# Modulation products with features on partitions: one multiply-and-sum per 128 features, all slots in the first two layers

## The chip, the cores and the metric

The kernel runs on one core of a Trainium2 chip. The metric is the time of one execution on the device in microseconds (us). All data are 32-bit floats. Five engines work side by side and are tied together by semaphores: TensorE (PE; its weight loads are PEld), VectorE (DVE), ScalarE (ACT), GpSimd (POOL) and SyncE (SP), which here issues the loads.

## The reference

Four transformer layers run over one sequence of 256 tokens with 1024 features: a gated-MLP layer, a chunked-attention layer, an "even" layer (forgetting and sliding-window attention) and an "odd" layer (sparse attention and eight experts). The last two are modulated by a vector `c`:

```python
def ada_modulation(c, w, b):                      # c [1, 1024], w [1024, 6144]
    mod = jax.nn.silu(c) @ w + b
    return jnp.split(mod[:, None, :], 6, axis=-1)

def even_layer(x, c, ...):                        # odd_layer likewise
    sh_m, sc_m, g_m, sh_f, sc_f, g_f = ada_modulation(c, ada_w, ada_b)
    h = rms_norm(x, norm_mix) * (1 + sc_m) + sh_m
    ...
    x = x + g_m * mix
    h = rms_norm(x, norm_ffn) * (1 + sc_f) + sh_f
    return x + g_f * swiglu(h, ffn_gate, ffn_up, ffn_down)
```

The two modulation matrices hold 6144 x 1024 numbers each, 50 MB together. Neither depends on the tokens.

## The kernel before

**The stream.** All weights come as one list of slots, each up to 128 x 2048 numbers (1 MB), in the order in which they are used. `Plan` writes the list. SyncE loads slot s into `raw[s % 6]` (`load`, L371); before it reuses a place it waits until TensorE has used the weights there (`w_used`) or, for a modulation slot, until VectorE is done with it (`lo_done`). ScalarE rounds a weight slot to its high part (`whi`, L1135), VectorE subtracts it to get the low part (`wlo`, `split`, L1679). TensorE makes each product as three matmuls (L449 to L451) from the high and low parts of activations and weights. A product of 512 columns from 1024 rows takes two weight slots; a "chunk" is such a product for both halves of 128 tokens.

**The order of the stages** is gmlp_in, gmlp_out, up0, down0 (the first layer's feed-forward block), kv, q, attn_out, up1, down1, e_in, e_out, e_up, e_down (even layer), o_in, o_out and the experts.

**Modulation slots** ("a") stand between the weight slots, at the places that `behind` names for each stage. There are 48 of them, 24 for each modulated layer. Slot n of a layer holds four blocks of 128 rows of the matrix for 512 output features, so two slots make 512 features. When `split` has made the low part of the weight slot in front of it, it calls `modulate`, which multiplies the rows on the partitions by silu(c) and adds: four operations of 128 x 512 into `acc` (L1703, L1705), each waiting for the one before. The sum over the 128 partitions is left to TensorE: `ada_turn` waits for the second slot of the pair and makes four matmuls of `acc` with a column of ones into bank 4 of PSUM (L665). `ada_cols` (L1727) adds the bias and stores 512 features as four columns of 128. Because bank 4 serves other purposes as well, the spatial product and the second scores of each attention wait for `ada_taken`. Of the 48 slots, 24 stand in the first two layers (none in up0 and up1) and 24 in e_in, e_out, e_up and e_down.

**The feed-forward block of the first two layers** (`conv_ffn`, `gated_ffn`). up0 and up1 are eleven chunks each. In one turn of the loop ScalarE copies the finished chunk out of PSUM (L1189), TensorE turns it (L614), ScalarE makes the convolution's first tap (L1285), VectorE adds two more taps in eight operations (L1930), ScalarE takes Silu (L1290), VectorE multiplies and splits (L1941, L1944, L1945). VectorE's instructions run in the order of the program: the low parts of the next chunk's two slots come first in a turn, then the convolution of the chunk before. down0 and down1 take 12 weight slots; the last low parts for them are interleaved with the last two turns of the convolution, and the first of these stand in this order:

```python
evac()                                    # low parts of the first two slots of down
convolve(j, lambda: split(used[0] + LEAD))     # the third, between taps and products
split(used[0] + LEAD + 1)                      # the fourth
convolve(n - 1, lambda: split(used[0] + LEAD + 2))   # the fifth
```

**Normalised projections.** Into e_in, e_up and o_in (`residual_normed`, `normed_product`) TensorE waits until VectorE and ScalarE have added the residual, normalised and scaled the first half of the tokens. VectorE adds the first half (t = 0) when that half of the last slot's product is done (`t0_done`); ahead of it it splits two more weight slots.

Of the kernel before, what the change touches and what calls it, by code (L numbers as in the profile page):

```python
# [22 lines left out]
ALU = mybir.AluOpType  # L23
# [54 lines left out]
C_C = C_AB + 2 * 6 * KT  # L78
C_END = C_C + KT

# [20 lines left out]
class Plan:  # L101
# [3 lines left out]
    def __init__(self):  # L105
        self.width, self.kind, self.q, self.at, self.qat, self.ada = [], [], [], {}, {}, []
        self.nq = 0
        left = [ADA, ADA]

        def add(widths, layer=None, behind=()):  # L110
            for i, w in enumerate(widths):
# [4 lines left out]
                if i in behind:  # L116
                    n = ADA - left[layer]
                    left[layer] -= 1
# [3 lines left out]
                    self.ada.append((len(self.kind) - 1, layer, n))  # L122
# [4 lines left out]
        def proj(name, n, order=None, kt=KT, layer=None, behind=(), first=None):  # L127
# [5 lines left out]
            add([k * w for (_, w), ks in zip(chunks_of(n, order), parts) for k in ks], layer, behind)  # L133
# [14 lines left out]
        assert not left[0]  # L148
# [4 lines left out]
        assert not left[1]  # L153
# [37 lines left out]
def build_program(nc, x_in, cols_in, rows_in, vg_in, fg1_in, fg_in, pos_in, ws_in, toep_in, rw_in, stream_in, out):  # L191
# [3 lines left out]
    with ctx:  # L195
# [35 lines left out]
        cs = sb("cs", [P, KT])  # L231
        acc = sb("acc", [P, W])
# [110 lines left out]

        neg_max, total, sink, weight = ((lambda u, t, c=c: sx[:, u // 4 % 2, c, t, u % 4:u % 4 + 1]) for c in range(4))
        parts = lambda t: slice(t * P, t * P + (t + 1) * P)

        def turned_before(name):

            return sum(n % 2 for s, _, n in PL.ada if s < AT[name])

# [2289 lines left out]
```

## Time and profile before

| what | us |
|---|---|
| median of 3 runs | 1512.16 |
| lowest and highest run | 1512.07, 1515.78 |
| span of the profiled execution, first to last instruction | 1509.6 |
| median of the runs, beyond that span | 2.6 |
| TensorE busy in the span | 1447.0 |
| VectorE busy | 1220.9 |
| ScalarE busy | 899.8 |
| data moved | 356.15 MB, 236 GB/s on the mean |

The page gives no time for the profiled execution but its span, so the sum further down is made against the span. Times in the profile are counted from the span's start. "Busy" leaves out waits; matmuls overlap, so a matmul's duration (0.39 us for 512 columns) is longer than the time to the next one (0.23 us). The stages follow each other: up0 begins at 93 us, down0 at 224, kv at 290, q at 340, attn_out at 391, up1 at 416, down1 at 547, e_in at 618, e_up at 734, e_down at 865 and o_in at 936 us.

### The profile page before, as it was taken

To read this page: it belongs to the slowest core of one execution; us is meant where nothing else is said; L and a number is where in the kernel's file an instruction comes from. 1 tells how busy PE (TensorE), PEld (TensorE's weight loads), DVE (VectorE), ACT (ScalarE), POOL (GpSimd) and SP (SyncE) were. 2 spreads that over 40 slices of the span, in tenths; PEclk is the share of its full clock that TensorE was granted. 3 is DMA by queue.
4 is the path that set the end of the run, shared out by engine and by line. 5 is a ranking of instruction groups with operands and counts; after the bars stand their busy time and mean duration, and the time that the engine had idled before them with its cause. 6 is when DMAs were issued, how large, how long until landed. Compare 5 with 4: busy or idle time off the path is not lost.

```text
span 1509.6 us, 19548 instructions
## 1 busy us (share of the span) xinstructions
PE 1447.0 (96%) x7128; PEld 1186.0 (79%) x7129; DVE 1220.9 (81%) x1664; ACT 899.8 (60%) x1207; POOL 5.6 (0%) x18
## 2 busy tenths in 40 slices
PE   6999999999999999998999999979899999999996
PEld 5888888887688887886788887856788888888885
DVE  6776879767767889878878788697688998999897
ACT  6555664556656563567433334547676777787774
POOL 0000000000000000000000000000000000000000
PEclk9999999999999999999999999979899999999999
DMA  8565446875355457561576676421289898998883
GB/s 298 226 231 187 169 172 231 331 269 222 112 199 188 157 181 294 212 247 58 200 272 253 261 314 239 162 89 61 118 324 340 329 337 319 340 354 324 330 332 152
DMA packets 53422, 356.15 MB, mean 236 GB/s; under 512 B 6096, under 2 KB 7120, under 8 KB 12896
## 3 DMA queue, kind: packets, MB, share of 16 engines
q1 hardware_dynamic: 52592, 352.15, 62.7%
q0 software_dynamic: 320, 2.65, 0.5%
q8 instruction: 49, 0.80, 0.2%
q10 hardware_dynamic: 432, 0.30, 0.1%
q14 instruction: 29, 0.24, 0.0%
HBM read 354.03 MB, written 1.05 MB: 235 GB/s over the span
## 4 chain that ended last, share of the span: by engine, by line
PE 77%; DVE 13%; ACT 6%; DMA 2%; issue 2%; SPq 0%; DVEq 0%; ACTq 0%
PE ps L449 23%; PE ps L451 22%; PE ps L450 22%; DVE wlo L1679 4%; DMA raw<-stream_dram 2%; PE ps L614 1%; ACT attn_scratch L1321 1%; PE ps L541 1%; ACT whi L1135 1%; PE ps L665 1%; DVE acc L1705 1%; DVE tok L1930 1%; ACT tok L1342 1%; DVE xlo L1769 1%; DVE tok L1864 1%
## 5 line engine op out<-in xcount | busy, mean ns | idle before, releaser
L1679 DVE TENSOR_TENSOR wlo<-raw,whi 128x2048 fp32r<-128x2048 f32 (+2 forms) x302 | 645.2, 2163 | 90.4 <-ACT whi L1135 79.0
L1135 ACT ACTIVATE whi<-raw 128x2048 fp32r<-128x2048 f32 (+2 forms) x302 | 541.1, 1816 | 173.9 <-DMA raw<-stream_dram 169.0
L449 PE MATMUL ps<-whi,xhi 128*128 128x512 f32 (+3 forms) x1360 | 533.8, 392 | 14.1 <-DVE xlo L1859 4.2
L451 PE MATMUL ps<-whi,xlo 128*128 128x512 f32 (+3 forms) x1360 | 522.5, 384 | 0.0
L450 PE MATMUL ps<-wlo,xhi 128*128 128x512 f32 (+3 forms) x1360 | 521.8, 384 | 0.0
L449 PEld LDWEIGHTS ps<-whi,xhi 128*128 128x128 f32 x1360 | 256.8, 189 | 70.4 <-issue 8.0
L451 PEld LDWEIGHTS ps<-whi,xlo 128*128 128x128 f32 x1360 | 256.9, 189 | 51.4
L450 PEld LDWEIGHTS ps<-wlo,xhi 128*128 128x128 f32 x1360 | 257.4, 189 | 46.5
L449 PE MATMUL ps<-whi,ahi 128*128 128x512 f32 x440 | 176.5, 401 | 1.4 <-DVE wlo L1679 1.3
L451 PE MATMUL ps<-whi,alo 128*128 128x512 f32 x440 | 173.7, 395 | 0.0
L450 PE MATMUL ps<-wlo,ahi 128*128 128x512 f32 x440 | 173.6, 395 | 0.0
L1705 DVE SCALAR_TENSOR_TENSOR acc<-raw,cs,acc 128x512 f32<-128x512 f32 x168 | 126.2, 751 | 5.1
L1930 DVE SCALAR_TENSOR_TENSOR tok<-ps,cols,tok 128x255 f32<-128x255 f32 (+1 forms) x176 | 72.7, 475 | 41.1 <-ACT tok L1285 40.3
L449 PEld LDWEIGHTS ps<-whi,ahi 128*128 128x128 f32 x440 | 83.0, 189 | 22.1 <-issue 2.6
L451 PEld LDWEIGHTS ps<-whi,alo 128*128 128x128 f32 x440 | 82.9, 188 | 19.2
L450 PEld LDWEIGHTS ps<-wlo,ahi 128*128 128x128 f32 x440 | 83.0, 189 | 17.8
L1189 ACT ACTIVATE tok<-ps,st 128x512 f32<-128x512 f32 x64 | 40.5, 685 | 55.5 <-PE ps L614 35.9
L1290 ACT ACTIVATE tok<-tok 128x512 f32<-128x512 f32 x22 | 13.9, 632 | 65.6 <-DVE tok L1930 65.6
L1554 ACT ACTIVATE tok<-ps 128x256 f32<-128x256 f32 (+1 forms) x48 | 17.4, 363 | 49.6 <-PE ps L451 49.4
L1285 ACT ACTIVATE tok<-ps,cols 128x256 f32<-128x256 f32 x88 | 42.5, 575 | 3.8 <-DVEq L1948 3.8
L1321 ACT ACTIVATE attn_scratch<-attn_scratch,sx 128x128 f32<-128x128 f32 x80 | 35.3, 445 | 10.0 <-DVE sx L2011 9.9
L1305 ACT ACTIVATE tok<-ps 128x512 f32<-128x512 f32 x11 | 6.6, 598 | 52.9 <-PE ps L451 52.9
(316 smaller groups left out, 1166.1 us busy)
## 6 DMA issues: line engine op xcount, KB each, us to landing
raw<-stream_dram SPq DMA_DIRECT2D x315, 1024.0 KB, 4.9
raw<-stream_dram SPq DMA_DIRECT2D x32, 512.0 KB, 3.9
attn_scratch<-toep_dram POOLq DMA_DIRECT2D x1, 2048.0 KB, 11.7
raw<-stream_dram SPq DMA_DIRECT2D x2, 528.0 KB, 4.5
h<-x_dram SPq DMA_DIRECT2D x2, 512.0 KB, 4.7
y<-tok SPq DMA_DIRECT2D x4, 256.0 KB, 2.7
head_scratch<-w_s_dram SPq DMA_DIRECT2D x1, 512.0 KB, 13.9
head_scratch<-vg_dram SPq DMA_DIRECT2D x1, 512.0 KB, 11.0
```

The costliest lines, as they stand in the source:

```text
L449: pe.matmul(o, xh, wh, start=start, stop=False)
L450: pe.matmul(o, xh, wl, start=False, stop=False)
L451: return pe.matmul(o, xl, wh, start=False, stop=stop)
L541: last = pe.transpose(trb(n % 2)[0:src.shape[1], k - r, t * P:(t + 1) * P], src, ident[:, :])
L1135: act.activation(whi[:, q % SPL, 0:w], raw[:, s % RAW, 0:w], ACT.Copy).then_inc(sem("hi_done"), 1)
L1189: m = act.activation(dst[:, t], src[:, t], func, scale=st[:, 6 + t:7 + t])
L1285: m = act.activation(conv[:, f, :], ps[:, 6 + f // 2, (f % 2) * S:(f % 2 + 1) * S], ACT.Identity, scale=sc, bias=bi)
L1321: m = act.activation(x, x, ACT.Exp, bias=neg_max(u, t), scale=-1.0, accum_out=total(u, t))
L1554: act.activation(sgx[:, 0:m], ps[:, (2, 0, 1)[j % 3], m:2 * m], ACT.Silu).then_inc(sem("x_silu"), 1)
L1679: dve.tensor_tensor(low(q)[:, 0:w], raw[:, s % RAW, 0:w], whi[:, q % SPL, 0:w].bitcast(F32), ALU.subtract).then_inc(sem("lo_done"), 1)
L1705: m = dve.scalar_tensor_tensor(acc[:, :], wk, cs[:, kk:kk + 1], acc[:, :], ALU.mult, ALU.add)
L1930: m = dve.scalar_tensor_tensor(o, src, cols[:, c:c + 1], o, ALU.mult, ALU.add)
```

## The change

A modulation slot now holds two blocks of 128 output features for all 1024 rows, features on the partitions and rows along them. silu(c) is kept as a row of 1024 on every partition (`c_row`, in the half of `gates` that is free in these layers), loaded by one more broadcast DMA behind slot 8, and taken through Silu by ScalarE at the head of `conv_ffn(0)`. Each block is one `tensor_tensor_reduce` of 128 x 1024, which multiplies, sums along the row, starts from the bias and writes one column of `shf2`, `scl2` or `gcol`. The product itself is written over the slot.

TensorE's part goes (`ada_turn`, its semaphores, its waits in front of the spatial product and the scores), and so do `acc`, `ada_cols`, `take_cols` and the deferral of a slot at the end of attention (`hold`, `owed`). `1 + scale`, times the norm's gain, is made once for all, behind the last slot; the gate turns wait for `modulated`. All 48 slots stand in the first two layers: 10 in up0, 8 in down0, 8 in kv, 3 in q, 11 in up1 and 8 in down1. gmlp_in, gmlp_out, attn_out and all stages of the even layer have none.

```diff
-        proj("gmlp_in", 2 * D, G_ORDER, layer=0, behind=(4, 5), first=FIRST)
-        proj("gmlp_out", D, layer=0, behind=odd)
-        proj("up0", 2 * FF)
-        proj("down0", D, kt=FK, layer=0, behind=(4, 5, 7, 8, 10, 11))
-        proj("kv", 2 * D, layer=0, behind=(2, 3, 5, 7))
-        proj("q", D, layer=0, behind=(1, 2))
-        proj("attn_out", D, layer=0, behind=odd)
-        proj("up1", 2 * FF)
-        proj("down1", D, kt=FK, layer=0, behind=(4, 5, 7, 8, 10, 11))
-        proj("e_in", E_IN, E_ORDER, layer=1, behind=(3, 5, 7, 8))
-        proj("e_out", D, layer=1, behind=odd)
-        proj("e_up", 2 * FF, layer=1, behind=odd[1:])
-        proj("e_down", D, kt=FK, layer=1, behind=(1, 2, 4, 5, 7, 8, 10, 11))
+        early = (0, 1, 2, 3, 4, 6, 7, 8)
+        proj("gmlp_in", 2 * D, G_ORDER, first=FIRST)
+        proj("gmlp_out", D)
+        proj("up0", 2 * FF, behind=odd[1:])
+        proj("down0", D, kt=FK, behind=early)
+        proj("kv", 2 * D, behind=range(8))
+        proj("q", D, behind=range(3))
+        proj("attn_out", D)
+        proj("up1", 2 * FF, behind=odd)
+        proj("down1", D, kt=FK, behind=early)
+        proj("e_in", E_IN, E_ORDER)
+        proj("e_out", D)
+        proj("e_up", 2 * FF)
+        proj("e_down", D, kt=FK)
...
+                if s == 8:
+                    sp.dma_start(c_row, c_in.to_broadcast([P, D])).then_inc(sem("c_landed"), 16)
...
-                    ada_turn(PL.s_of[q] + 1)
...
-            def ada_turn(s):
-                if (s, turned[0] // (ADA // 2), 2 * (turned[0] % (ADA // 2)) + 1) not in PL.ada:
-                    return
-                if turned[0]:
-                    pe.wait_ge(sem("ada_taken"), turned[0])
-                pe.wait_ge(sem("lo_done"), s + 1)
-                for j in range(4):
-                    m = pe.matmul(ps[:, 4, j:j + 1], acc[:, j * P:(j + 1) * P], ones[:, 0:1], start=True, stop=True)
-                m.then_inc(sem("ada_cols"), 1)
-                turned[0] += 1
...
+                if layer == 0:
+                    act.wait_ge(sem("c_landed"), 16)
+                    act.activation(c_row, c_row, ACT.Silu).then_inc(sem("cs"), 1)
                 evac(first=True)
...
-                    act.activation(cs[:, :], cols[:, C_C:C_C + KT], ACT.Silu).then_inc(sem("cs"), 1)
...
             def modulate(s):
...
                 dve.wait_ge(sem(f"landed{s % RAW}"), 16 * (s // RAW + 1))
-                for k in range(4):
-                    kk = 4 * (n % 2) + k
-                    wk = raw[:, s % RAW, k * W:(k + 1) * W]
-                    if kk == 0:
-                        m = dve.tensor_scalar(acc[:, :], wk, cs[:, 0:1], None, ALU.mult)
-                    else:
-                        m = dve.scalar_tensor_tensor(acc[:, :], wk, cs[:, kk:kk + 1], acc[:, :], ALU.mult, ALU.add)
-                    if k < 3 or n % 2 == 0:
-                        link(m)
...
+                for b in range(2):
+                    blk = 2 * n + b
+                    part, kind, k = blk // (3 * KT), blk // KT % 3, blk % KT
+                    wk = raw[:, s % RAW, b * D:(b + 1) * D]
+                    at = C_AB + layer * 6 * KT + blk
+                    m = dve.tensor_tensor_reduce(wk, wk, c_row, 1.0, cols[:, at:at + 1], ALU.mult, ALU.add,
+                                                 (shf2, scl2, gcol)[kind][:, layer, part, k:k + 1])
+                m.then_inc(sem("lo_done"), 1)
+                if seen[0] == 2 * ADA:
+                    dve.wait_ge(sem("lo_done"), s + 1)
+                    for part in range(2):
+                        at = (C_GEM, C_GEF)[part]
+                        x = scl2[:, :, part, :]
+                        g = cols[:, at:at + 4 * KT].rearrange("p (l r) -> p l r", l=2)[:, :, 0:KT]
+                        m = dve.scalar_tensor_tensor(x, x, 1.0, g, ALU.add, ALU.mult)
+                    m.then_inc(sem("modulated"), 1)
...
-                split(used[0] + 2, hold=True)
+                split(used[0] + 2)
```

## Rows read from the trace of the kernel before

**Rows 1.** The page: busy time, GB/s in 40 slices, chain that ended last.
```profile
PE 1447.0 (96%) x7128; PEld 1186.0 (79%) x7129; DVE 1220.9 (81%) x1664; ACT 899.8 (60%) x1207; POOL 5.6 (0%) x18
...
GB/s 298 226 231 187 169 172 231 331 269 222 112 199 188 157 181 294 212 247 58 200 272 253 261 314 239 162 89 61 118 324 340 329 337 319 340 354 324 330 332 152
...
PE 77%; DVE 13%; ACT 6%; DMA 2%; issue 2%; SPq 0%; DVEq 0%; ACTq 0%
```
**Rows 2.** Waits from 126.48 to 221.47 us: total, times, longest.
```profile
DVE tok L1930 <- ACT tok L1285: 10.5, 8, 1.4
```
**Rows 3.** Stretches: length, then busy us of each engine, clock, DMA share, GB/s.
```profile
126.48:221.47 94.99, 94.99 (x450) 78.85 (x449) 76.89 (x104) 58.67 (x73) 0.00 (x0) 1.00 0.49 172
290.16:340.03 49.87, 49.61 (x242) 40.96 (x241) 34.16 (x40) 27.99 (x36) 1.49 (x2) 1.00 0.79 296
1057.00:1120.00 63.00, 57.01 (x281) 47.66 (x281) 45.93 (x66) 41.59 (x54) 0.53 (x1) 0.92 0.53 203
```
**Rows 4.** VectorE's timeline, one turn in up0: start, length, idle before.
```profile
126.48 4.50 DVE L1679 TENSOR_TENSOR wlo<-raw,whi 128x2048 fp32r<-128x2048 f32 x2
132.19 3.34 DVE L1930 SCALAR_TENSOR_TENSOR tok<-ps,cols,tok 128x255 f32<-128x255 f32 x8 [1.22 <-ACT tok L1285]
...
138.25 4.49 DVE L1679 TENSOR_TENSOR wlo<-raw,whi 128x2048 fp32r<-128x2048 f32 x2
```
**Rows 5.** VectorE's timeline where down0 begins.
```profile
221.47 3.43 DVE L1679 TENSOR_TENSOR wlo<-raw,whi 128x1024 fp32r<-128x1024 f32 x2
227.19 3.34 DVE L1930 SCALAR_TENSOR_TENSOR tok<-ps,cols,tok 128x255 f32<-128x255 f32 x8 [2.30 <-ACT tok L1285]
...
247.90 2.29 DVE L1679 TENSOR_TENSOR wlo<-raw,whi 128x2048 fp32r<-128x2048 f32 x1
```
**Rows 6.** Groups by form: count, then busy us, mean ns, idle before.
```profile
L1705 DVE SCALAR_TENSOR_TENSOR acc<-raw,cs,acc 128x512 f32<-128x512 f32 x168 | 126.2, 751 | 5.1
...
L1679 DVE TENSOR_TENSOR wlo<-raw,whi 128x1024 fp32r<-128x1024 f32 x32 | 39.1, 1223 | 6.1 <-ACT whi L1135 4.5 <-DVE alo L2401 0.9
...
L665 PE MATMUL ps<-ones,acc 128*128 128x1 f32 x192 | 22.7, 240 | 0.0
...
L1703 DVE TENSOR_SCALAR acc<-raw,cs 128x512 f32<-128x512 f32 x24 | 11.5, 479 | 0.0
```
**Rows 7.** TensorE's timeline around one column group in down0.
```profile
270.85 0.95 PE L665 MATMUL ps<-ones,acc 128*128 128x1 f32 x8
271.65 0.48 PE L449 MATMUL ps<-whi,ahi 128*128 128x512 f32 x1
```
**Rows 8.** Timelines at two exits: last matmul of the first half, VectorE's add.
```profile
723.59 0.39 PE L451 MATMUL ps<-whi,xlo 128*128 128x512 f32 x1
...
726.63 0.69 DVE L1790 TENSOR_TENSOR tok<-ps,gates 128x512 f32<-128x512 f32 x1
...
927.09 0.39 PE L451 MATMUL ps<-whi,alo 128*128 128x512 f32 x1
...
928.52 0.69 DVE L1790 TENSOR_TENSOR tok<-ps,gates 128x512 f32<-128x512 f32 x1
```
**Rows 9.** VectorE's timeline: `tensor_tensor_reduce` (add, minimum) in the chunked attention.
```profile
361.76 0.29 DVE L2011 CUSTOM_DVE_ANT_0 attn_scratch<-ps,attn_scratch 128x128 f32<-128x128 f32 x1 [0.63 <-PE ps L690]
...
361.98 0.42 DVE L2011 CUSTOM_DVE_ANT_0 attn_scratch<-ps,attn_scratch 128x256 f32<-128x256 f32 x1
362.32 0.08 DVE L2011 DVE_READ_ACCUMULATOR2_ANT sx<- 128x1 f32 x1
362.32 0.28 DVE L2011 CUSTOM_DVE_ANT_0 attn_scratch<-ps,attn_scratch 128x128 f32<-128x128 f32 x1
```
**Rows 10.** TensorE's timeline at the second slot of q.
```profile
347.50 0.50 PE L449 MATMUL ps<-whi,xhi 128*128 128x512 f32 x1 [1.29 <-DVE xlo L1769]
```
**Rows 11.** ScalarE's timeline ahead of up0.
```profile
90.37 1.06 ACT L1142 ACTIVATE tok<-h 128x1024 f32<-128x1024 f32 x1 [0.52 <-DVE h L1788]
...
98.06 1.28 ACT L1224 ACT_TABLE_LOAD   x1
```
**Rows 12.** DMA issues: count, KB each, us to landing.
```profile
attn_scratch<-toep_dram POOLq DMA_DIRECT2D x1, 2048.0 KB, 11.7
...
head_scratch<-vg_dram SPq DMA_DIRECT2D x1, 512.0 KB, 11.0
```

More of the change, by code:

```diff
@@ L107, in __init__, with add @@
         self.nq = 0
-        left = [ADA, ADA]
-        def add(widths, layer=None, behind=()):
+        def add(widths, behind=()):
             for i, w in enumerate(widths):
@@ L132, in proj @@
                 parts[0] = first
-            add([k * w for (_, w), ks in zip(chunks_of(n, order), parts) for k in ks], layer, behind)
+            add([k * w for (_, w), ks in zip(chunks_of(n, order), parts) for k in ks], behind)
         def expert():
@@ L692, in scores, with first_scores, attention @@
                 m.then_inc(sem("att_s"), 1)
-            def first_scores(units, name):
+            def first_scores(units):
                 pe.wait_ge(sem("acc_free"), T("acc"))
                 scores(units, 0)
-                cols_made = turned_before(name)
-                if cols_made:
-                    pe.wait_ge(sem("ada_taken"), cols_made)
                 scores(units, 1)
-            def attention(units, name, sm, pT, after=None, mid=None, between=lambda: None):
+            def attention(units, sm, pT, after=None, mid=None, between=lambda: None):
                 n = len(units) // 2
@@ L783, in spatial @@
                     pe.wait_ge(sem("acc_free"), 3)
-                    pe.wait_ge(sem("ada_taken"), 1)
                     for g in range(KT):
@@ L830, in last_queries @@
                 pe.wait_ge(sem("tr_free"), T("tr"))
-            attention(CHUNKED, "attn_out", SM_C, PT_C, lead(2), between=last_queries)
+            attention(CHUNKED, SM_C, PT_C, lead(2), between=last_queries)
             gated_ffn(4, rest(3))
@@ L861, in fox_heads @@
                     pe.wait_ge(sem("tr_free"), T("tr", 1))
-                    first_scores(EVEN, "e_out")
+                    first_scores(EVEN)
             def fox_keys():
@@ L871, in _ @@
             proj(width[4], after=fox_heads)
-            attention(EVEN, "e_out", SM_E, PT_E, between=fox_keys)
+            attention(EVEN, SM_E, PT_E, between=fox_keys)
             gated_ffn(2, normed=True)
@@ L1663, in _, with split @@
             seen = [0]
-            owed = [None]
-            def split(n, i=None, per=0, hold=False):
-                if owed[0] is not None:
-                    modulate(owed[0])
-                    owed[0] = None
+            def split(n, i=None, per=0):
                 while pos[0] < min(n, top[0]):
@@ L1681, in split @@
                     if s + 1 < len(PL.kind) and PL.kind[s + 1] == "a":
-                        if hold and pos[0] == n:
-                            owed[0] = s + 1
-                        else:
-                            modulate(s + 1)
+                        modulate(s + 1)
             def modulate(s):
-                _, layer, n = PL.ada[seen[0]]
-                assert PL.ada[seen[0]][0] == s
+                at, layer, n = PL.ada[seen[0]]
+                assert at == s
+                if seen[0] == 0:
+                    dve.wait_ge(sem("cs"), 1)
@@ L2150, in _ @@
             dve.wait_ge(sem("bias_ready"), 1)
-            attention(CHUNKED, "attn_out", SM_C, PT_C)
+            attention(CHUNKED, SM_C, PT_C)
             residual_then()
@@ L2190, in _ @@
             T.up("tr", 11)
-            attention(EVEN, "e_out", SM_E, PT_E)
+            attention(EVEN, SM_E, PT_E)
             residual_normed(KT, 0, 0, 1)
```

75 lines of the change are left out of this document (17 added, 58 removed).

## The prediction

> **What bounds the kernel now.** I read the page first, then the waits of one long stage, then that stage's timeline on VectorE, then the two ends of each feed-forward block. The page [rows 1] says that TensorE is busy 96% of the span and that the chain which ended last lies on it for 77% and on VectorE for 13%. So work taken off TensorE is nearly all worth its length, and work given to VectorE counts only where the chain runs through VectorE. The question is where that is.
>
> In the first feed-forward block, from 126.48 to 221.47 us, TensorE is busy 94.99 of 94.99 us and VectorE 76.89 [rows 3]. That looks like 18 us of room on VectorE. It isn't. The timeline [rows 4] shows one turn of the loop, two weight slots long: two `wlo` subtractions, an idle stretch, eight convolution steps, a short wait for Silu, three short steps, and at 138.25 the next `wlo`. The 94.99 us hold 8 turns, 11.87 each. The waits [rows 2] tell what the idle time is: 10.5 us in 8 times, 1.31 us a turn, until ScalarE has made the convolution's first tap, and that is the only part which a later VectorE could use up. The other idle pieces come behind VectorE's own work and move with it. Each `wlo` that starts a turn ends right as TensorE comes for it: both loops are equally long. Work put into a turn is free up to 1.31 us and costs its full length beyond.
>
> The end of such a block is tighter still. From 221.47 to 247.90 VectorE alternates `wlo`, convolution and products, with one idle stretch, the 2.30 us at 227.19 [rows 5], and TensorE starts on each slot as it is finished.
>
> **What is taken away.** Each of 24 output blocks of 512 features has its partial products summed across partitions by four matmuls with one column (`ada_turn`), recorded as 192 [rows 6]. One group takes 0.80 us of TensorE, from 270.85 to 271.65, where the next weights start [rows 7]. All 24 would be 19.2 us. Four of them win nothing by themselves: those ahead of the three normalised projections, where TensorE waits for VectorE anyway, and the one in `gmlp_in`, behind which the next start is set by the chain that makes `vn_ready`. 20 remain: **-16.0**.
>
> The three exits into a normalised projection get shorter too, as no modulation slot is in the way there. In `e_out` VectorE comes to the add at 726.63, right behind its last `wlo`, although the half of the product that the add reads was done at 723.98; at `e_down` the add comes at 928.52 and the half is done at 927.48 [rows 8]. An add follows a finished product by some 0.2 us, so 2.4 us and 0.8 us go. The exit of `down1` is built like that of `e_down` and its `wlo` waits for a weight slot behind two modulation slots: I count 1.1. Together **-4.3**.
>
> **What VectorE gets.** Two products of 128x1024 for each of 48 slots, in place of four of 128x512 (0.78 us from start to start, 0.751 long, so 3.05 to 3.1 a slot) [rows 6]. The same operation is in the trace at 128 and 256 elements: behind each other they start 0.22 and 0.34 us apart, the accumulator's readout included [rows 9]. That is about 0.135 us for each 128 more, so 0.22 + 7 x 0.135 = 1.16 us for 1024, and **2.3 us a pair** (call it p). The upper bound is two full lengths, 1.223 for a two-input product of that size [rows 6] and 0.08 for the readout: 2.61. The lower bound, were it to run like a one-input operation, is 1.5, as 512 elements of those took 0.48 against the 0.75 of the two-input ones [rows 6]. I take 2.3, since the row is the same operation.
>
> The Trainium skill (VectorE: DVE Perf Modes, The DRAIN you can't avoid) says that the next operation doesn't start until the pipeline is empty. The trace disagrees for this operation: one that lasts 0.42 us is followed after 0.34. By the page a pair would cost 2.61 and the sum below would be 8 us longer.
>
> **Where it gets them.** The slots move: none before `up0`, then 10, 8, 8, 3, 0, 11 and 8 in `up0`, `down0`, `kv`, `q`, `attn_out`, `up1` and `down1`, and none after.
>
> *`up0` and `up1`.* They had none. Now one stands behind the second slot of nearly each turn, between `wlo` and the convolution: 2.3 - 1.31 = 0.99 us a turn. Eight turns of each block are in the tight loop; the others fall in its start, where VectorE is idle for 7 us. 2 x 8 x 0.99 = **+15.8**. Nothing later gives it back: TensorE can't start a slot before its `wlo`.
>
> *`down0` and `down1`.* Five slots stand right behind the first five weight slots. The first two, 4.6 us, fall before the idle 2.30 and cost 2.3; the next two cost 2.3 each; the fifth replaces one that was there before (3.05, ahead of the `wlo` at 247.90) and wins 0.75. That makes 5p - 5.35 = 6.15 us for each, **+12.3**. The three in the second half have room: the `wlo` there is 2 to 6 us early.
>
> *`kv` and `q`.* In `q` a slot now precedes the split of the activations. TensorE was already held there, 1.29 us before its second slot, by that split [rows 10]; two pairs of 2.3 take the place of one group of 3.05: +1.6. In `kv` the stream is one modulation slot for each weight slot, 8 of each, beside the 2 MB of the bias table [rows 12]: 18.9 MB in about 47 us, 400 GB/s, where this stretch now moves 296 GB/s [rows 3] and the page's best slice shows 354 [rows 1]. At 1.05 MB a slot that is 53 us at 354; the six-slot ring hides some. +3 (0 to 6). Together **+4.6**.
>
> *The silu of c*, now 128x1024 on ScalarE at the head of `up0`, before two weight copies: 1.28 for a table and some 1.06 for the operation, as another one of that size takes [rows 11], of which some half is covered, as `wlo` there was about 1 us early: **+1.2**. The one in `gmlp_in` that goes had room behind it. The load of c itself lies among loads that land long before use: nothing. If that cover were gone it would be the 11.0 us that the like load of `vg` takes [rows 12]. The waits for `ada_taken` ahead of the scores and the spatial product go with the groups. The last two operations, which turn all scales at once, are a few tenths on VectorE in `down1`'s second half, with room.
>
> **Sum.** -16.0 - 4.3 + 15.8 + 12.3 + 4.6 + 1.2 = +13.6 us. The profiled execution's span is 1509.6, so 1523.2; the median of the runs, 1512.16, lies 2.6 above that span, and the prediction is **1525.8 us**. As a function of p the sum is 26p - 46 (16 turns and five slots in each of two block ends): each tenth of a us on a pair is 2.6 us, it is zero at p = 1.77, and +21.6 at 2.61.
>
> **The rivals.**
> 1. *Faster: the product fits into the wait.* Were a pair 1.5 us, the turns would cost 0.2 each and the sum were -7: 1505. It decides at 1.77 us a pair. For it: the operations with one tensor input do run faster. Against: this one reads two, and its own rows give 0.135 us per 128. A sum below zero could also come of a smaller loss at the ends of the blocks. 12%.
> 2. *No change: the ends of the blocks don't lose.* Were `down0` and `down1` to take the five slots without a loss, because TensorE's wait for the last hidden blocks moves no further, the sum is +1: 1513. Against it: VectorE has no idle time there but the 2.30. 13%.
> 3. *Each product pays its full length*, p = 2.61, or the stream in `kv` costs 9 us more than counted here: 1534. This is also what the page on VectorE gives. Against it: [rows 9]. 15%.
> 4. *The clock falls.* TensorE would be busy 11.75 of 12.86 us a turn, 91%. In [rows 3] a stretch with 90% (57.01 of 63) showed a granted clock of 0.92. A clock of 0.92 would lengthen a turn's TensorE work to 12.8, just what the turn lasts; only below that does it cost, some 1 us a turn at 0.85, so 16 turns make 1541. 5%.
> The forecast has 55%, its own range 1519 to 1531.
>
> **The numbers.** A measurement can tell about 0.3%, 4.5 us, from no change. Faster by more than that (below 1507.6): 12%. Within: 15%, rival 2 and part of the forecast's low side. Slower: 73%. The range from 1511 to 1537 leaves out rival 1 and the far side of 3 and 4.
>
> **What would show it.** The second product of a pair starts 1.16 us behind the first, and 2.3 us lie between `wlo` and the next operation. In `up0` and `up1` the wait of the convolution for ScalarE is gone from VectorE, the turn is 12.86 us instead of 11.87, and TensorE waits about 1 us a turn for `wlo`. `up0` with `down0` takes 14 us more up to the start of `down0`'s second half, and so does `up1` with `down1`. From the end of `down1` to the start of `o_in`'s product the kernel is 12 us shorter: 10 groups and the three exits. Wrong it would be if the pair is far from 2.3, if `kv` starves on the stream, or if TensorE's clock falls in the feed-forward blocks.

## The result, and the profile after

The changed kernel takes 1527.98 us (median of 4 runs, 1527.58 to 1528.86); the kernel before, beside it, 1512.24 (1512.07 to 1515.78). The ratio is 1.0104, with an interval from 1.0087 to 1.0122: it is slower by 1%. The prediction was 1525.8 us, slower.

The page of the changed kernel, as in [rows 1] and [rows 6]:

```profile
PE 1434.2 (94%) x6936; PEld 1165.9 (76%) x6937; DVE 1198.1 (78%) x1634; ACT 895.8 (59%) x1205; POOL 5.6 (0%) x18
...
PE 64%; DVE 24%; ACT 6%; issue 4%; DMA 2%; SPq 0%; DVEq 0%; ACTq 0%
...
L1667 DVE CUSTOM_DVE_ANT_0 raw<-raw,gates,cols 128x1024 f32<-128x1024 f32 x96 | 119.2, 1279 | 0.0
```

TensorE has 12.8 us less to do and VectorE 22.8 us less. The program is 15.7 us longer all the same, because VectorE's share of the chain that ended last has risen from 13 to 24%: its work was made smaller and put where nothing covers it. The timeline of VectorE shows it for one turn in up0, the turn of [rows 4]:

```profile
139.21 4.49 DVE L1649 TENSOR_TENSOR wlo<-raw,whi 128x2048 fp32r<-128x2048 f32 x2
143.62 1.28 DVE L1667 CUSTOM_DVE_ANT_0 raw<-raw,gates,cols 128x1024 f32<-128x1024 f32 x1
144.82 0.08 DVE L1667 DVE_READ_ACCUMULATOR2_ANT shf<- 128x1 f32 x1
144.82 1.28 DVE L1667 CUSTOM_DVE_ANT_0 raw<-raw,gates,cols 128x1024 f32<-128x1024 f32 x1
146.03 0.08 DVE L1667 DVE_READ_ACCUMULATOR2_ANT shf<- 128x1 f32 x1
146.03 3.33 DVE L1875 SCALAR_TENSOR_TENSOR tok<-ps,cols,tok 128x255 f32<-128x255 f32 x8
...
152.09 2.29 DVE L1649 TENSOR_TENSOR wlo<-raw,whi 128x2048 fp32r<-128x2048 f32 x1
```

The pair takes from 143.62 to 146.03, 2.41 us; the convolution follows without the idle time that it had in [rows 4]; the turn lasts 12.88 us (139.21 to 152.09) instead of 11.87, the mean of the eight turns in [rows 3]. TensorE's waits over eight such turns (139.21 to 242.30 us), and its busy time there:

```profile
PE ps L442 <- DVE wlo L1649: 8.0, 8, 1.6
```
```profile
139.21:242.30 103.09, 95.10 (x448) 77.69 (x446) 95.89 (x138) 58.02 (x73) 0.00 (x0) 1.00 0.65 250
```

TensorE was busy for all of the 94.99 us in [rows 3]. For the same work it now needs 103.09, of which 95.10 are work and 8.0 are eight waits for `wlo`. The granted clock is 1.00, the upper of its two levels (2.4 GHz): it isn't the clock.

**Where the 17.5 us of span went.** I compared the time at which TensorE starts on each weight slot in both traces. The shift at a stage's start, after minus before: up0 -1.2, down0 +7.4, kv +12.4, q +15.3, attn_out +13.8, up1 +13.0, down1 +21.5, e_in +26.4, e_up +22.3, e_down +18.0, o_in +14.3, o_out's last slot +15.9, end of the program +17.5. Between neighbouring slots the shift gives each term:

| term | predicted | measured |
|---|---|---|
| column groups off TensorE | -16.0 | -16.9 |
| exits of down1, e_out, e_down | -4.3 | -4.3 (1.05, 2.35, 0.88) |
| up0 and up1, up to the first slot of down0, down1 | +15.8 | +14.7 (7.6, 7.1) |
| first half of down0 and down1 | +12.3 | +15.4 (7.5, 7.9) |
| kv and q | +4.6 | +3.0 |
| silu of c | +1.2 | +1.0 |
| second slot of up1 | 0 | +1.3 |
| half clock in o_in | 0 | +1.6 |
| the experts | 0 | +1.6 |
| sum | +13.6 | +17.4 |

The first half of down0 in VectorE's timeline, which answers to [rows 5]:

```profile
229.76 1.22 DVE L1649 TENSOR_TENSOR wlo<-raw,whi 128x1024 fp32r<-128x1024 f32 x1
230.90 1.28 DVE L1667 CUSTOM_DVE_ANT_0 raw<-raw,gates,cols 128x1024 f32<-128x1024 f32 x1
...
233.31 2.29 DVE L1649 TENSOR_TENSOR wlo<-raw,whi 128x2048 fp32r<-128x2048 f32 x1
...
237.93 3.33 DVE L1875 SCALAR_TENSOR_TENSOR tok<-ps,cols,tok 128x255 f32<-128x255 f32 x8
...
262.80 3.43 DVE L1649 TENSOR_TENSOR wlo<-raw,whi 128x2048 fp32r<-128x2048 f32 x2
```

VectorE has no idle time here. It begins the block 8.29 us later than before (229.76 against 221.47) and makes the low part that stood at 247.90 [rows 5] at 262.80, 14.90 later: 6.6 us for five slots, as 5p - 5.35 = 6.7 says at p = 2.41. TensorE's first start in down0 moved by only 7.4, since that low part had been 1.0 us early. So 0.9 us of each block end in the table belongs to the turns: 16.5 for the turns and 13.6 for the two ends. In down1 VectorE's part was 6.4 us (sixth low part at 571.02 before, at 599.79 now; start of the block 22.37 later); some 0.6 us more came from a stretch at half clock, shown in the last section.

The last two rows of the table don't come from anything that the change edits. From o_out's last slot to the end, which is the experts, the two kernels do the same, in 452.5 us before and 454.2 now. It took between 451.1 and 456.9 in the eight kernels up to `old_clear` below, whichever way their slots lay, and 451.1 and 454.7 in two executions of one and the same kernel (`old_clear`); a profile of one execution cannot tell 2 us there from nothing.

### The profile page after: what moved, and what is told of

Read it like the earlier page. It is cut to its first block, busy times and chain, and to the rows that moved or that the text cites. A ratio compares the mean times of both kernels' runs of the same rounds, so it can differ in the third digit from the quotient of the medians.

```text
span 1527.1 us, 19080 instructions
## 1 busy us (share of the span) xinstructions
PE 1434.2 (94%) x6936; PEld 1165.9 (76%) x6937; DVE 1198.1 (78%) x1634; ACT 895.8 (59%) x1205; POOL 5.6 (0%) x18
## 3 DMA queue, kind: packets, MB, share of 16 engines
HBM read 354.55 MB, written 1.05 MB: 233 GB/s over the span
## 4 chain that ended last, share of the span: by engine, by line
PE 64%; DVE 24%; ACT 6%; issue 4%; DMA 2%; SPq 0%; DVEq 0%; ACTq 0%
PE ps L442 19%; PE ps L444 19%; PE ps L443 19%; DVE wlo L1649 7%; DVE tok L1875 5%; DVE raw L1667 5%; DMA raw<-stream_dram 2%; ACT attn_scratch L1298 1%; PE ps L533 1%; ACT whi L1109 1%; DVE alo L1890 1%; DVE tok L1886 1%; ACT tok L1264 1%; DVE ahi L1889 1%; ACT tok L1319 1%
## 5 line engine op out<-in xcount | busy, mean ns | idle before, releaser
L442 PE MATMUL ps<-whi,xhi 128*128 128x512 f32 (+3 forms) x1360 | 534.1, 393 | 32.1 <-DVE wlo L1649 16.5
L1667 DVE CUSTOM_DVE_ANT_0 raw<-raw,gates,cols 128x1024 f32<-128x1024 f32 x96 | 119.2, 1279 | 0.0
L1927 DVE TENSOR_TENSOR tok<-ps,tok 128x512 f32<-128x512 f32 x11 | 7.6, 692 | 46.1 <-ACT tok L1282 41.3
```

The lines of the kernel that those rows point to most:

```text
L442: pe.matmul(o, xh, wh, start=start, stop=False)
L1667: m = dve.tensor_tensor_reduce(wk, wk, c_row, 1.0, cols[:, at:at + 1], ALU.mult, ALU.add, (shf2, scl2, gcol)[kind][:, layer, part, k:k + 1])
```

## The experiments

**`one_product`: the second product of a pair cut to 8 of its 1024 rows, in up0 and up1 alone.** (The kernel leaves out the rest of these sums, so some modulation values are incomplete.)

```diff
+                    short = b and (AT["up0"] <= s < AT["down0"] or AT["up1"] <= s < AT["down1"])
+                    r = slice(0, 8 if short else D)
-                    m = dve.tensor_tensor_reduce(wk, wk, c_row, 1.0, cols[:, at:at + 1], ALU.mult, ALU.add,
+                    m = dve.tensor_tensor_reduce(wk[:, r], wk[:, r], c_row[:, r], 1.0, cols[:, at:at + 1], ALU.mult, ALU.add,
```

> In up0 and up1 the second product of each modulation slot runs over 8 of its 1024 rows only; loads, order and all else are as in the changed kernel (some modulation values are therefore partial sums). Theory A (a turn of the loop costs what VectorE gets beyond the 1.31 us in which it waited before): a pair takes some 2.34 us in the changed kernel, here about 1.17 + 0.17 = 1.34, so the turn falls from 12.9 to about 11.9 us and the time by 16 x 1.0 = 16 us, to 1512 us. Rival B (the third slot of the stream in each turn, its transfer and its place in the ring, makes the turn longer): the turn stays at 12.9 and the time at 1528 us.

Measured: 1510.21 us (1507.41 to 1513.27, 10 runs) beside 1513.09 for before; ratio 0.9982, 0.9971 to 0.9994. VectorE's timeline of a turn, then TensorE's waits over eight turns (138.07 to 233.00 us):

```profile
138.07 4.49 DVE L1649 TENSOR_TENSOR wlo<-raw,whi 128x2048 fp32r<-128x2048 f32 x2
142.48 1.28 DVE L1669 CUSTOM_DVE_ANT_0 raw<-raw,gates,cols 128x1024 f32<-128x1024 f32 x1
...
143.68 0.22 DVE L1669 CUSTOM_DVE_ANT_0 raw<-raw,gates,cols 128x8 f32<-128x8 f32 x1
...
143.96 3.34 DVE L1877 SCALAR_TENSOR_TENSOR tok<-ps,cols,tok 128x255 f32<-128x255 f32 x8
...
150.02 2.29 DVE L1649 TENSOR_TENSOR wlo<-raw,whi 128x2048 fp32r<-128x2048 f32 x1
```
```profile
PE ps L442 <- DVE wlo L1649: 0.5, 1, 0.5
```

One product and a stub last 1.48 us, 0.17 over the wait of 1.31, and the turns are back: 0.5 us of waits instead of 8.0. 21 shorter products are some 18 us off the time (the ratio went from 1.0104 to 0.9982), because 16 of them lay in turns that VectorE paces. It also shows the margin: half a slot fits into a turn of up0 or up1, a whole one doesn't.

**`down_late`: the slots of down0 and down1 away from the convolution.**

```diff
-        early = (0, 1, 2, 3, 4, 6, 7, 8)
+        early = range(4, 12)
```

> The eight slots of down0 and of down1 stand behind weight slots 4 to 11 in place of 0 to 4 and 6 to 8. Theory A (they cost where VectorE's low parts alternate with the last two turns of the convolution, 7.5 us in each of the two blocks by the traces): the start of the sixth weight slot moves back by 7 us in each, at the price of about 1 us at the exit of down1 and up to 5 us of waiting for the stream, which then has one modulation slot for each weight slot through the end of down0, kv and q: 1514 to 1519 us. Rival B (VectorE has too much to do in the whole of down0 and down1, wherever it stands): the loss moves to the second half, 1526 to 1528 us.

Measured: 1528.23 us (1524.61 to 1531.86, 4 runs); ratio 1.0092, 1.0073 to 1.0112, no better than the changed kernel. My time of 1514 to 1519 was missed, though its mechanism held: the first half of down0 now loses nothing (shift of TensorE's start from down0's first slot to its sixth -0.4 us instead of +7.5, and -0.6 instead of +7.9 in down1). It was given back behind: some 2.5 us at the eighth and ninth slot of each block, 3.9 at the entry of kv, 1.0 at that of q and 7.2 at the entry of e_in; 1.3 more went in q's first slot, where the clock was at half speed from 353.2 to 360.0 us (mean 0.50). The time is that of rival B, but only the 2.5 us a block lie in the second half, where B had put the loss. VectorE's timeline at that last place, in `down_late` and then in the changed kernel:

```profile
631.13 2.29 DVE L1649 TENSOR_TENSOR wlo<-raw,whi 128x2048 fp32r<-128x2048 f32 x1 [0.69 <-ACT whi L1109]
635.39 2.29 DVE L1649 TENSOR_TENSOR wlo<-raw,whi 128x2048 fp32r<-128x2048 f32 x1 [1.96 <-ACT whi L1109]
...
637.96 0.69 DVE L1733 TENSOR_TENSOR h<-ps,h 128x512 f32<-128x512 f32 x1
```
```profile
630.73 2.29 DVE L1649 TENSOR_TENSOR wlo<-raw,whi 128x2048 fp32r<-128x2048 f32 x1 [1.95 <-ACT whi L1109]
...
636.69 0.69 DVE L1733 TENSOR_TENSOR h<-ps,h 128x512 f32<-128x512 f32 x1 [3.43 <-PE ps L444]
```

In the changed kernel VectorE is through with its low parts and waits 3.43 us for TensorE, then adds at once. In `down_late` the products of the last slots have pushed the low parts behind the finished half of the product, and the residual add follows a low part with no idle time ahead of it. From TensorE's last matmul of down1 to its first product of e_in it is 12.2 us instead of 5.1.

**`clear_of_split`: no slot ahead of the split of the activations.**

```diff
-        proj("kv", 2 * D, behind=range(8))
-        proj("q", D, behind=range(3))
-        proj("attn_out", D)
-        proj("up1", 2 * FF, behind=odd)
+        proj("kv", 2 * D, behind=(0, 2, 3, 4, 5, 6, 7))
+        proj("q", D, behind=range(4))
+        proj("attn_out", D, behind=(1,))
+        proj("up1", 2 * FF, behind=odd[1:])
```

> The modulation slots behind the second weight slot of kv and of up1 are moved to the end of q and to attn_out. In the changed kernel TensorE waits 1.4 us longer than before in front of that weight slot in both stages. Theory A (the pair of products stands ahead of VectorE's split of the second half of the activations): both waits go, -2.9 us, 1525.1 us. Rival B (the longer wait is one for the weights): they stay, and the time is 1528 us within 0.5.

It was made for a wait that I hadn't predicted. In kv of the changed kernel a pair of products stands between a low part and the split of the second half of the tokens, and the second slot waits for that split; VectorE's timeline, then TensorE's:

```profile
305.84 1.28 DVE L1667 CUSTOM_DVE_ANT_0 raw<-raw,gates,cols 128x1024 f32<-128x1024 f32 x1
...
308.38 0.41 DVE L1713 CAST xhi<-tok 128x512 fp32r<-128x512 f32 x1
308.82 0.69 DVE L1714 TENSOR_TENSOR xlo<-tok,xhi 128x512 fp32r<-128x512 f32 x1
```
```profile
308.71 0.39 PE L444 MATMUL ps<-whi,xlo 128*128 128x512 f32 x1
310.63 0.50 PE L442 MATMUL ps<-whi,xhi 128*128 128x512 f32 x1 [1.54 <-DVE xlo L1714]
```

Measured: 1528.78 us (1526.83 to 1530.81, 4 runs), ratio 1.0102, 1.0083 to 1.0121: the time didn't fall by the 2.9 expected. In the trace both waits are gone (the distance between the two matmuls fell from 1.92 to 0.47 us, and likewise in up1), 2.9 us together. Most of it came back where the slots went: 0.7 at q's second slot, 0.5 at its fourth, 0.8 at the second and third slot of attn_out, which now has a modulation slot. From kv's start to up1's second slot 0.9 us are left. O_out's last slot starts 1.7 us earlier than in the changed kernel, but 1.6 of that arose in o_in, where the stretch at half clock was 3.4 us instead of 6.8 (last section), behind everything that was edited. Then the experts, which it doesn't touch, took 456.86 us against 454.15, by the stretches of the two kernels:

```profile
1071.24:1528.10 456.86, 437.05 (x2080) 361.07 (x2079) 396.73 (x375) 328.85 (x371) 0.53 (x1) 0.98 0.80 297
```
```profile
1072.95:1527.10 454.15, 435.43 (x2080) 359.90 (x2079) 397.54 (x375) 327.71 (x371) 0.53 (x1) 0.98 0.80 299
```

So the wait is real and was removed in the trace; moving its slots to these places was worth 0.9 us in the trace, and the measured time cannot tell that from nothing, since 1 or 2 us drown in the experts' scatter.

**`placed`: all 48 slots still in the first two layers, but where I thought that there was room.** Half slots in the turns of up0 and up1, down0 and down1 as in `down_late`, the rest in gmlp_in, gmlp_out, kv, q and attn_out.

```diff
+        proj("gmlp_in", 2 * D, G_ORDER, first=FIRST, behind=(8,))
+        proj("gmlp_out", D, behind=(0, 1, 2, 3))
+        proj("up0", 2 * FF, behind=(3, 5), halves=(7, 9, 11, 13, 15, 17, 19, 21))
+        proj("down0", D, kt=FK, behind=(4, 5, 6, 7, 8, 9, 10, 11))
+        proj("kv", 2 * D, behind=(0, 1, 2, 3, 4, 5, 6, 7))
+        proj("q", D, behind=(1, 2, 3))
+        proj("attn_out", D, behind=(0, 1, 2, 3))
```

> All together, the same computation: half slots (one product) in up0 and up1 except in two early turns each, eight late slots in down0 and down1, none behind the second weight slot of up1, slots in gmlp_in, gmlp_out and attn_out too, silu of c taken earlier in gmlp. Theory A (only VectorE's work beyond its idle time costs): against the changed kernel -16 for the turns, -15 for the block ends, -1.4 for up1, -1 for the silu, and up to +6 for the stream: 1495 to 1501 us, below the kernel before. Rival B (the total of VectorE's added work or the stream sets the time): above 1512 us.

Measured: 1519.95 us (1515.52 to 1524.90, 12 runs), ratio 1.0043, 1.0028 to 1.0058; slower than before, 19 us or more over what I expected. The turns did cost nothing (both blocks 0 us). The loss sits at the entries, in TensorE's waits up to the experts:

```profile
PE ps L444 <- DVE xlo L1716: 8.6, 4, 4.1
...
PE ps L557 <- DVE tok L1800: 6.1, 1, 6.1
...
PE ps L535 <- DVE h L1735: 3.1, 2, 2.1
```

The first is the split of the activations, the second the normalised half at e_in (a gap of 12.5 us there, as in `down_late`), the third a residual add ahead of up0 and another at the end of attn_out. The time is on rival B's side of 1512; the waits are those at the entries, which neither theory had. A slot at the end of one stage stands in VectorE's queue ahead of what the next stage waits for.

**`old_places`: the new operation at the places of the kernel before.** `c_row` gets a buffer of its own, so that it may live through the even layer. To make room, the convolution's coefficients move from `cols` into the free half of `gates`.

```diff
-        proj("up0", 2 * FF, behind=odd[1:])
+        proj("up0", 2 * FF)
...
+        proj("e_in", E_IN, E_ORDER, behind=(3, 5, 7, 8))
+        proj("e_out", D, behind=(1, 3))
+        proj("e_up", 2 * FF, behind=(3, 5, 7, 9, 11, 13, 15, 17, 19, 21))
+        proj("e_down", D, kt=FK, behind=(1, 2, 4, 5, 7, 8, 10, 11))
...
-        c_row = gates[:, 1, :]
+        c_row = sb("c_row", [P, D])[:, :]
+        cv = gates[:, 1, 0:C_CE]
```

> The new products at the places of the kernel before (24 slots in the first two layers, none in up0 and up1, 24 in the even layer). For that silu(c) has a buffer of its own and is made in gmlp_in as before, the convolution's coefficients lie in the second half of gates until e_in, and each layer's scales are finished behind its 24th slot; the computation is the same. Theory A (the change loses only by where the slots stand, and gains by the column groups and the shorter products): 20 groups of 0.8 us less than before, some tenths more from products of 2.42 in place of 3.1 us, 1 us back for the longer silu: 1494 to 1498 us. Rival B (the form of the products costs, through a bigger read of a shared row or the accumulator's readout): 1512 us or more.

Measured: 1490.45 us (1489.40 to 1493.33, 4 runs) beside 1512.32; ratio 0.9851, 0.9832 to 0.9871. Without the new places the change is a gain of 22 us; the places of the changed kernel turn it into a loss. It was some 5 us better than expected; `shifted`, below, shows where most of these come from.

**`old_clear`: the same, with the slots moved off the three exits, those that lead into e_in, e_up and o_in.**

```diff
-        proj("up0", 2 * FF)
-        proj("down1", D, kt=FK, behind=(4, 5, 7, 8, 10, 11))
-        proj("e_out", D, behind=(1, 3))
-        proj("e_up", 2 * FF, behind=(3, 5, 7, 9, 11, 13, 15, 17, 19, 21))
-        proj("e_down", D, kt=FK, behind=(1, 2, 4, 5, 7, 8, 10, 11))
+        proj("up0", 2 * FF, behind=(3, 5))
+        proj("down1", D, kt=FK, behind=(4, 5, 7, 8))
+        proj("e_out", D)
+        proj("e_up", 2 * FF, behind=(3, 5, 7, 8, 9, 11, 12, 13, 15, 17, 19, 21))
+        proj("e_down", D, kt=FK, behind=(1, 2, 4, 5, 7, 8))
```

(up1 has `behind=(3, 5)` too.)

> As old_places, with the slots taken away from the exits into the three normalised projections (the last two of down1 and e_down and both of e_out) and put into the loose first turns of up0 and up1 and into e_up. Theory A (the exits lose 4 us to slots that stand close to them, and the first turns of up0 and up1 take slots for nothing): 3 to 4 us less than old_places, 1491 to 1494 us. Rival B (the exits are set by the normalisation alone, or slots in up0 and up1 cost wherever they stand): no less than old_places.

Measured: 1485.60 us (1480.69 to 1486.94, 5 runs), ratio 0.9809, 0.9787 to 0.9831; run a second time, as `old_clear_again`, 1483.24 (1482.98 to 1489.41), ratio 0.9812, 0.9793 to 0.9832. VectorE's add at the exit into e_in, first `old_places`, then `old_clear`:

```profile
597.42 2.29 DVE L1653 TENSOR_TENSOR wlo<-raw,whi 128x2048 fp32r<-128x2048 f32 x1 [1.96 <-ACT whi L1112]
...
600.00 0.69 DVE L1736 TENSOR_TENSOR h<-ps,h 128x512 f32<-128x512 f32 x1
```
```profile
592.20 2.29 DVE L1653 TENSOR_TENSOR wlo<-raw,whi 128x2048 fp32r<-128x2048 f32 x1 [1.97 <-ACT whi L1112]
...
597.92 0.69 DVE L1736 TENSOR_TENSOR h<-ps,h 128x512 f32<-128x512 f32 x1 [3.19 <-PE ps L446]
```

The three gaps on TensorE are 5.1, 4.9 and 4.9 us instead of 7.4, 5.8 and 9.0: 7.3 us in all, of which the ratio shows 0.4%, 6 us. With `crow_first`, below, whose time can't be told from it, it is the fastest of the versions tried, 27 to 30 us below the kernel before.

**`shifted` and `shifted_before`: the place of two buffers.** In `old_places` TensorE made a slot of down0 in 5.49 us where the changed kernel takes 5.60, with no wait in it and the clock at 1.00. Both read `ahi` and `alo`, and moving the coefficients had put these 1408 bytes lower in each partition. These two kernels move the coefficients alone, in the changed kernel and in the one before. The small buffers behind `cols` move along; `xhi`, `xlo`, `whi`, `wlo` and `raw` stay where they are in every kernel of this document, so of what these matmuls read only `ahi` and `alo` have moved.

```diff
-C_CW = 9 * KT
+C_BS = 9 * KT
+C_CW = 0
...
         lf = sb("head_scratch", [P, FK * S])[:, :]
+        cv = sb("conv_cols", [P, C_CE])[:, :]
```

> The changed kernel, only the 352 columns of convolution coefficients stand in a buffer of their own behind the two large scratch buffers, so that ahi and alo (with the scratch) lie 1408 bytes lower in each partition, as they do in old_places and old_clear. There the matmuls that read ahi and alo follow each other 0.2289 us apart, in the changed kernel 0.2333 (TensorE's timeline, three stretches each). Theory A, it is the place of these two buffers: spacing 0.229 here too, 1320 such matmuls x 4.4 ns = 5.8 us less, of which some 1 us lies in the first halves of down0 and down1, where TensorE waits for VectorE anyway: 4.5 to 5 us shorter, 1523. Theory B, it comes from what else runs at that time (the 48 slots at other places): spacing 0.233 and 1528, as the changed kernel.

> The kernel before with the same move of the convolution coefficients: ahi and alo 1408 bytes lower than in the kernel before, where the spacing is 0.2325 us. That is another place than in old_places (before still has acc and cs ahead of them, 2080 bytes). Theory A: the spacing changes with the place, to 0.229 if this place is a good one (5 us less, 1507), or stays near 0.2325 if it is not (1512). Theory B: 0.2325 and 1512 within 1 us.

Measured: `shifted` 1522.88 us (1519.33 to 1524.94, 6 runs), ratio 1.0065, 1.0049 to 1.0082; `shifted_before` 1507.38 (1502.52 to 1514.32, 8 runs), ratio 0.9967, 0.9948 to 0.9986. TensorE's starts on two neighbouring slots of down0, in the changed kernel and in `shifted`:

```profile
279.31 0.40 PE L442 MATMUL ps<-whi,ahi 128*128 128x512 f32 x1
...
284.91 0.40 PE L442 MATMUL ps<-whi,ahi 128*128 128x512 f32 x1
```
```profile
278.85 0.39 PE L444 MATMUL ps<-whi,ahi 128*128 128x512 f32 x1
...
284.34 0.39 PE L444 MATMUL ps<-whi,ahi 128*128 128x512 f32 x1
```

24 matmuls lie between the two: 5.60 us are 0.2333 each, 5.49 are 0.2288. 1320 such matmuls (528 of them in the experts) make 6 us, which the ratios show (1.0104 to 1.0065, 0.39%). The theory that it comes of the slots' places falls. The kernel before went at 0.2321, `old_places` at 0.2289: 1320 times 3.2 ns are 4 us. So of the 22 us of `old_places` about 4 belong to the buffers' place and 18 to the operation and the groups that it takes away. The same holds of the change itself, at 0.2333 against 0.2321: some 1 us of its loss, spread over the rows of the table, is the place of two buffers and not the slots.

**`crow_first` and `crow_pad`: which place?** `old_clear` with `c_row` ahead of `ahi`, without and with 32 bytes of padding.

```diff
+        c_row = sb("c_row", [P, D])[:, :]
+        pad = sb("pad", [P, 8])
         with nc.sbuf_tensor("ahi", [P, FK, S], F32R) as ahi, nc.sbuf_tensor("alo", [P, FK, S], F32R) as alo:
...
-        c_row = sb("c_row", [P, D])[:, :]
```

> old_clear with c_row, 4096 bytes, placed ahead of ahi and alo instead of behind the scratch buffers; nothing else changes. Counted from the place of ahi in the changed kernel, the spacing of the matmuls that read ahi and alo was 0.2333 us at 0, 0.2321 at +2080 bytes (the kernel before), 0.229 at -1408 (old_clear, shifted) and 0.2267 at +672 (shifted_before). This one is at +2688. Theory A, what counts is the place modulo 2048 bytes or a divisor of it: +2688 is 32 bytes off +672, spacing near 0.227, 2 to 3 us shorter than old_clear: 1481. Rival B, what counts is something else (distance to another buffer, or a larger modulus): anything between 0.2267 and 0.2333, so 1481 to 1491. The kernel before is fixed at 1512.

> crow_first with 32 bytes of padding ahead of ahi, so that it is at +2720, 2048 bytes from the place in shifted_before (0.2267 us). Theory A (modulo 2048): spacing 0.2267 exactly as in shifted_before, 1481. If crow_first and crow_pad differ by more than 1 ns of spacing, 32 bytes matter; if both are slow, the modulus is larger than 2048 or the rule is another.

Measured: `crow_first` 1484.94 us (1479.43 to 1490.54, 5 runs), ratio 0.9804, 0.9778 to 0.9830; `crow_pad` 1488.54 (1485.23 to 1492.10, 5 runs), ratio 0.9826, 0.9807 to 0.9846. The starts on two neighbouring slots of down0, first `crow_first`, then `crow_pad`:

```profile
267.35 0.39 PE L444 MATMUL ps<-whi,ahi 128*128 128x512 f32 x1
...
272.84 0.39 PE L444 MATMUL ps<-whi,ahi 128*128 128x512 f32 x1
```
```profile
267.68 0.40 PE L445 MATMUL ps<-whi,ahi 128*128 128x512 f32 x1
...
273.28 0.40 PE L445 MATMUL ps<-whi,ahi 128*128 128x512 f32 x1
```

A slot takes 5.49 us in the first, 5.60 in the second. The intervals of the two times overlap; the pace is what tells them apart. The modulus of 2048 that I had guessed was not tested, because I had counted two of the places wrong. The kernel before has `cs` (32 bytes) and `acc` (2048) ahead of `ahi`, and its `cols` is eight columns, another 32 bytes, longer. Counted from the changed kernel, its `ahi` lies at +2112 and not at +2080, and that of `shifted_before` at +704 and not at +672. `crow_pad`, at +2720, is therefore 2016 bytes from `shifted_before`, not 2048; the test needs 64 bytes of padding and was not run. No two of the six places contradict a modulus of 2048, and none shows it beyond the pair 4096 bytes apart. What stands: 32 bytes change the pace by 2%, and two places 4096 bytes apart (`old_clear` and `crow_first`) gave the same. The rule is open.

## Why the prediction was right

It was 2.2 us low, with the likeliest case and its mechanism: VectorE's longer turns and block ends cost more than TensorE wins. Signs that it named are there: from the fourth slot of up0 to the sixth of down0 the kernel lost 15.0 us, and as much from the fourth slot of up1 to the sixth of down1, for 14 forecast; and from e_in to o_in it won the 12 that had been said. By its own steps:

- **The groups and the exits.** Both held: -16.9 and -4.3 for -16.0 and -4.3. The three exits, of which one had been costed by likeness only (1.1 us for down1), measured 1.05, 2.35 and 0.88. From e_in to o_in the kernel gained 12.1 us more, with the exit of down1 13.1; 12 had been said, 8 for ten groups and 4.3 for the exits.
- **The price of a pair.** 2.3 us was worked out from the same operation at 128 and 256 elements, and it is 2.41: the step from one start to the next is 1.21 us, not 1.16. That it came so near is in part luck. The starts in [rows 9] are 0.22 and 0.34 us apart, which is 0.12 for each 128 more and not 0.135; from 0.12 a pair is 2.1 and the sum +9, 1521. From 256 to 1024 elements the step really grows by 0.145 for each 128. By 26p - 46 the step from 2.3 to 2.41 is 2.9 us (p also stands twice in the term of q, so it should be 28p); the two rows of the table in which p stands came out 2.0 over. The trace shows here too that an operation of 1.28 us is followed after 1.20, readout included. (By the Trainium skill, VectorE: DVE Perf Modes, The DRAIN you can't avoid, the second would start when the first is through; with the trace's 1.28 that gives an estimate of 2.56 and more for a pair. The trace disagrees. The same page, under Two Vector instructions with no wait between them, lets an operation that isn't held start before the one ahead of it has finished; with that the trace agrees, and the prediction had left it out.) Rival 3 falls on both its counts, and rival 1 as well, which needed 1.77.
- **The turns.** 1.31 us of cover a turn was nearly right: with p = 2.41 a turn should have grown by 1.10 us, and it grew by 1.01. `one_product` shows it from the other side: with 1.48 us in the place of 2.41, TensorE hardly waits, 0.5 us in eight turns.
- **The block ends.** Rival 2 falls: VectorE lost 6.6 us in down0 and 6.4 in down1, near the 6.7 of the formula. What the prediction missed is small: the low part at the head of down0 was 1.0 us early, so that 0.9 us of the turns' loss shows only inside the block.
- **kv and q.** The size was near (3.0 for 4.6), and half of it stood there for the wrong reason. The 3.0 are 1.3 in kv and, in q, 2.4 less 0.7. The part of q held, 1.7 for 1.6: a pair now stands right ahead of the split at q's entry, and TensorE's wait for that split has grown from 0.18 to 3.44 us, of which 0.8 only replace the column group that stood there (kernel before, then changed kernel):

```profile
340.03 0.50 PE L449 MATMUL ps<-whi,xhi 128*128 128x512 f32 x1 [0.18 <-DVE xlo L1769]
```
```profile
355.33 0.50 PE L442 MATMUL ps<-whi,xhi 128*128 128x512 f32 x1 [3.44 <-DVE xlo L1714]
```

The other part, +3 for a stream that keeps TensorE waiting, did not come. The stream did run at the rate that the prediction had taken for its most, 354 GB/s:

```profile
302.59:345.73 43.14, 41.60 (x197) 34.16 (x196) 34.87 (x43) 22.27 (x30) 1.49 (x2) 1.00 0.92 356
```

In that stretch the DMA engines were busy 92% of the time. From 302.59 to 355.33 us ScalarE waited four times for a load, 8.9 us in all. But the distances between kv's slots on TensorE stayed those of before but for one, less the one group that went: TensorE waited for none of it. The one distance that grew, 1.3 us, is the pair ahead of the split of the activations, which the prediction had seen in q [rows 10] and not looked for in kv and in up1, where it costs 1.3 to 1.4 us each.

- **The clock.** Rival 4 falls for the feed-forward blocks: 1.00 over eight turns with TensorE busy 92% of the time (the 11.75 us of work a turn that the rival took are 11.87 by [rows 3], so 92% and not 91). The 1.6 us in o_in are a stretch at 0.5 that was twice as long as before, behind no edit of the change.
- **From the span to the time.** I added 2.6 us for what lies beyond the span, from the median of the runs. The profiled execution of the changed kernel is 1.8 us beyond its own span (1528.86 and 1527.1), so 0.8 too much. The sum, +13.6, was 3.9 us short of the 17.5 of the traces. Of these 3.9 the 0.8 hid one part, and another 0.9 is that the profiled execution was slower than the median of the runs. That the miss shrank to 2.2 is luck. And 3.2 of what the sum lacked are the half clock in o_in and the experts, which no edit of the change touches.

What was argued and not tried: the cover of the silu of c, measured at 1.0 us in the shifts alone.

## What to carry to other kernels

An operation that is cheaper in itself is worth its saving only at a place with cover. Here the same product gained 22 us at the old places (about 4 of them from where two buffers came to lie) and lost 15 at the new ones. Before work is moved into a stage, don't look at the busy share of its engine; look for a wait that the work can use up, in a turn, and for what stands behind the place in the engine's queue: a split, a residual add or a normalisation that another engine waits for is delayed by whatever is ahead of it (a pair of 2.41 us cost 2.4 at q's entry, and 1.3 in kv and in up1). A loss moved out of one wait is to be looked for at the next entry before the time is believed, as `down_late` shows.

## What the runs showed of the hardware

- **The pace of matmuls depends on where their operands lie in a partition.** Same instruction, same clock, no wait: 0.2267 us (5.44 a slot of 24), 0.229, 0.232 and 0.2333, four values in six places of `ahi` and `alo`; in up0 of the changed kernel those with `xhi` and `xlo` went at 0.2267 (24 from 143.09 to 148.53 us). Two of the places differ by 32 bytes and by 2%.
- **The multiply-and-sum of 128x1024 lasts 1.28 us and is followed after 1.21**, with a readout of 0.08 that lies within; of 128x8, 0.22 and 0.15.
- **Short stretches at half clock come and go with edits elsewhere.** Of the changed kernel, 4 us in down1, where 2.66 us had just passed from one matmul to the next, 2.26 of them a wait for a low part:

```profile
595.50:599.50 4.00, 3.91 (x10) 3.12 (x11) 3.93 (x7) 2.43 (x2) 0.00 (x0) 0.57 1.04 436
```

A mean of 0.57 is 3.4 of the 4 us at the lower of the two levels, 1.2 GHz. The kernel before has none there; nor has the same wait in down0 of the changed kernel one. Most of it was absorbed: in down0 the next slot waited for its low part, 1.20 us from matmul to matmul, and in down1 it didn't, 0.23, so that of the 7.9 us of down1 some 0.6 are the clock's. In o_in nothing absorbs it. The stretch at half clock there, in the changed kernel and in the one before, by the windows:

```profile
967.90:974.70 6.80, 6.80 (x24) 5.83 (x24) 5.44 (x7) 3.20 (x5) 0.00 (x0) 0.50 0.44 154
```
```profile
954.20:957.60 3.40, 3.40 (x13) 2.92 (x13) 2.81 (x3) 2.23 (x3) 0.00 (x0) 0.50 0.43 157
```

3.4 us more at half the pace are 1.7 us lost, the 1.6 of the table. Two executions of `old_clear` show the same stretch in o_in, 6.8 us long, from 927.8 and from 927.4 us, so there it goes with the kernel and not with chance; in the experts one of the two has a stretch of 3.4 us at 1251.7 that the other lacks. What makes such a stretch come or grow was not tried.
